# Seven half products for the down projections of two of three SwiGLU groups, in one sequence with the up pairs

## What is computed

```python
def swiglu(x, wg, wu, wd):
    hid = jax.nn.silu(jnp.einsum('btd,df->btf', x, wg)) * jnp.einsum('btd,df->btf', x, wu)
    return jnp.einsum('btf,fd->btd', hid, wd)

x = layer_norm(ALPHA * x + 0.5 * swiglu(x, ffn1_wg, ffn1_wu, ffn1_wd), ln1_g, ln1_b)
...
x = layer_norm(ALPHA * x + 0.5 * swiglu(x, ffn2_wg, ffn2_wu, ffn2_wd), ln3_g, ln3_b)
```

## Time and profile before

| | us |
|---|---|
| median of 3 runs (1088.27 to 1089.12) | 1088.27 |
| the profiled execution's own time | 1087.43 |
| its span | 1085.6 |
| TensorE matmul busy (8731 matmuls) | 1054.4 |
| VectorE busy | 688.7 |
| GpSimd busy | 525.6 |
| ScalarE busy | 437.2 |

### The profile page before, as it was taken

How to read it: one execution, slowest core, us unless ns; L and a number is a source line. 1 busy time by engine, 2 the same in 40 slices (tenths; PEclk the granted TensorE clock), 3 DMA queues, 4 the chain that set the end, 5 groups by cost and what they waited for, 6 DMA issues and landing times.

```text
span 1085.6 us, 20864 instructions
## 1 busy us (share of the span) xinstructions
PE 1054.4 (97%) x8731; PEld 1047.7 (97%) x8731; DVE 688.7 (63%) x1019; ACT 437.2 (40%) x658; POOL 525.6 (48%) x311
## 2 busy tenths in 40 slices
PE   8899999999999988999999999989999999999996
PEld 7899999999999988999999999988999999999996
DVE  6999921288846865342625427989996016886486
ACT  4565532155553443222231324445555113555234
POOL 4355654154568246444453546324565433566321
PEclk9999999999999999999999999999999999999999
DMA  8134234233355042242342335103334323433402
GB/s 256 36 102 117 77 100 117 78 100 116 98 137 136 15 108 75 68 117 72 90 117 67 114 93 144 40 2 97 114 94 125 88 69 98 117 99 88 121 26 79
DMA packets 195002, 103.30 MB, mean 95 GB/s; under 512 B 4420, under 2 KB 193428, under 8 KB 194901
## 3 DMA queue, kind: packets, MB, share of 16 engines
q1 hardware_dynamic: 194827, 101.85, 33.0%
q10 hardware_dynamic: 82, 0.12, 0.1%
HBM read 99.74 MB, written 2.48 MB: 94 GB/s over the span
## 4 chain that ended last, share of the span: by engine, by line
PE 85%; DVE 10%; issue 2%; ACT 2%; DMA 1%; POOL 0%; SPq 0%; ACTq 0%; DVEq 0%; POOLq 0%
PE ps L1303 14%; PE ps L1323 14%; PE ps L1320 14%; PE ps L1321 14%; PE ps L1305 14%; PE ps L1304 14%; DVE x L1179 1%; DVE xl L925 1%; DVE x L1160 1%; DVE form_lo L976 1%; DMA raw<-in_ffn_wd_dram 1%; DMA xrow<-in_x_prompt_dram 1%; PE ps L1426 1%; PE ps L1366 1%; PE ps L1416 0%
## 5 line engine op out<-in xcount | busy, mean ns | idle before, releaser
L569 POOL TENSOR_TENSOR wl<-raw,wh 128x512 fp32r<-128x512 f32 x120 | 221.6, 1874 | 226.2 <-DVE raw L951 182.3
L615 ACT ACTIVATE wh<-raw 128x1024 fp32r<-128x1024 f32 (+3 forms) x203 | 238.4, 1178 | 191.9 <-DMA raw<-in_ffn_wd_dram 102.2
L1303 PE MATMUL ps<-form_hi,wh 128*128 128x260 f32 x640 | 182.3, 285 | 5.1 <-ACT temps L615 5.1
L1305 PE MATMUL ps<-form_hi,wl 128*128 128x260 f32 x640 | 181.6, 284 | 0.0
L1304 PE MATMUL ps<-form_lo,wh 128*128 128x260 f32 x640 | 181.6, 284 | 0.0
L1320 PE MATMUL ps<-xh,wh 128*128 128x260 f32 x640 | 167.9, 283 | 3.8 <-DVE ymix L1253 3.8
L1321 PE MATMUL ps<-xl,wh 128*128 128x260 f32 x640 | 167.3, 283 | 0.0
L561 POOL TENSOR_TENSOR wl<-raw,wh 128x1536 fp32r<-128x1536 f32 (+2 forms) x36 | 108.1, 3010 | 107.1 <-ACT wh L615 107.1
L1320 PE MATMUL ps<-hid_hi,wh 128*128 128x260 f32 x544 | 141.9, 282 | 0.0
L1321 PE MATMUL ps<-hid_lo,wh 128*128 128x260 f32 x544 | 141.8, 283 | 0.0
L1303 PE MATMUL ps<-xh,wh 128*128 128x260 f32 x480 | 136.8, 285 | 2.1 <-DVE temps L983 1.5
(11 more groups left out here) (225 smaller groups left out, 2354.7 us busy)
## 6 DMA issues: line engine op xcount, KB each, us to landing
raw<-in_ffn_wg_dram SPq DMA_DIRECT2D x80, 256.0 KB, 3.3
raw<-in_w_in_dram SPq DMA_DIRECT2D x40, 512.0 KB, 3.9
raw<-in_ffn_wd_dram SPq DMA_DIRECT2D x16, 768.0 KB, 5.7
b<-in_ffn_wu_dram SPq DMA_DIRECT2D x40, 256.0 KB, 3.4
raw<-in_ffn_wu_dram SPq DMA_DIRECT2D x40, 256.0 KB, 3.0
raw<-in_ffn_wd_dram SPq DMA_DIRECT2D x16, 640.0 KB, 5.4
raw<-in_w_out_dram SPq DMA_DIRECT2D x7, 512.0 KB, 3.9
xrow<-in_x_prompt_dram SPq DMA_DIRECT2D x4, 512.0 KB, 5.3
```

What stands on the lines that cost most here:

```text
L569: nc.gpsimd.tensor_tensor(wl_slot[:, s, :], raw_slot[:, s, :], wh_slot[:, s, :].bitcast(F32), ALU.subtract).then_inc(lo_ready, 1)
L615: return nc.scalar.activation(out, in_, ACT.Copy)
L1303: mm(out, hi, vh, start=start and n == 1, stop=False, skip_group_check=more)
L1305: ins = mm(out, lo, vh, start=False, stop=n == count, skip_group_check=more)
```

## The change

The 22 hidden tiles form three groups of 8, 6 and 8. The down products of the first two groups become units of the same form as the up pairs: a unit takes two output tiles (2j, 2j+1) and treats the group's even and odd hidden tiles as the two halves of the inner dimension. Seven half products of four blocks (group 0) or three (group 1) take the place of eight. Up pairs and down units stand in one list, `UNITS`, of NU = 28, numbered p: 1 to 7 are hidden tiles 2 to 8; 8 to 11 the down units of group 0; 12 to 17 hidden tiles 9 to 14; 18 to 21 the down units of group 1; 22 to 28 hidden tiles 15 to 21. One stream of two slot sets serves all of them. The last group's down products stay full, with 8 blocks a chunk; chunks are placed in two slots and split in two halves by GpSimd.

For the down units the moving operands are made from hidden tiles in VectorE's turns: hid_hi and hid_lo become several tensors (one, two, mid, late, and the second token half of xh and xl for the fourth form, with its fp32 in xl32, which now has memory of its own), and `mid_sums` and `mid_rest` make the forms of tiles 1 to 7 and 9 to 13. The results go straight into x32 (`down_first`, `down_second`, `down_fourth`), where the copies kept by ScalarE carry the 0.5. Silu is one ScalarE instruction, and the products L983, L1012 and L1016 are gone. ScalarE rounds T1 and T3 first, then the loaded blocks, then T2 and T4; before it was the loaded blocks, then T1 and T3, then T2 and T4. The scaling of the residual is spread by SCALED_IN. In the diff the first `unit_steps` is ScalarE's and the second VectorE's.

```diff
-    SPANS = ((2, 12), (12, KF))
-    HELD = (12, KF - 12)
+    GROUPS = (8, 6, 8)
+    UNITS = [None]
+    for g in range(len(GROUPS)):
+        for f in range(max(GROUP_AT[g], 2), GROUP_AT[g] + GROUPS[g]):
+            UNITS.append(("up", f))
+            if g and f == GROUP_AT[g]:
+                UNITS += [("down", g - 1, j) for j in range(K // 2)]
...
         def in_halves(what):
-            return what[0] in ("mix", "out") and size_of(what) == K
+            return (what[0] in ("mix", "out") or what[1] == "down") and size_of(what) >= 6
...
+            def load_unit(n, p):
+                if UNITS[p][0] == "up":
...
+                else:
+                    _, g, j = UNITS[p]
+                    k0, k1 = GROUP_AT[g], GROUP_AT[g] + GROUPS[g]
+                    b11, b21 = (column(wd_v[n], 2 * j)[:, k0 + i:k1:2, :] for i in range(2))
+                    b12_, b22 = (column(wd_v[n], 2 * j + 1)[:, k0 + i:k1:2, :] for i in range(2))
+                load_half(n, "B11", p, b11)
+                if unit_no(n, p) > 2:
+                    sp.wait_ge(t13_made, unit_no(n, p) - 2)
...
                 def hid_up(f, pair):
                     act.wait_ge(s.hid_made, f + 1)
-                    copy(two(hid_hi[:, f % HELD[0], :]), pair_of(pair)).then_inc(s.hid_round, 1)
+                    if f == 0:
+                        act.wait_ge(w_used, number[n, "open", 3])
+                    i = (f - GROUP_AT[group_of(f)]) // 2
+                    if group_of(f) < LAST_GROUP and f % 2 == 0:
+                        copy(one_hi[:, one_at(f), :], bank(pair, 0))
+                        ins = copy(even32[:], pair_of(pair))
+                    elif group_of(f) < LAST_GROUP:
+                        ins = copy(two_hi[:, :, i, :], pair_of(pair))
...
+                def unit_steps(p):
...
+                    act.wait_ge(w_used, number[n, "P1", p])
+                    keep(first_p, x_bank, 1, p_taken)
+                    act.wait_ge(w_used, number[n, "Q5", p])
+                    keep(first_q, z_bank, 1, q_taken)
+                    if p < NU:
+                        round_thirteen(n, p + 1)
...
+                    if was[0] == "up":
+                        second_gate(p - 1)
+                    if p < NU:
+                        round_unit(n, p + 1)
...
+                    act.wait_ge(w_used, number[n, "P6", p])
+                    keep(first_u, x_bank, -1, u_taken)
+                    if was[0] == "up":
+                        hid_up(was[1], p % 2)
+                    if p < NU:
+                        round_twenty_four(n, p + 1)
+                    if was[0] != "down":
+                        round_mid(was[1])
+                    if not down:
+                        act.wait_ge(p_taken, no)
+                        nc.scalar.activation(bank((p + 1) % 2, 0), gate_sum, ACT.Silu).then_inc(s.on1, 1)
...
+            SCALED_IN = {2: (0, 1), 4: (2, 3), 6: (4,), 8: (5,), 9: (6,), 10: (7,)}
...
+                def fourth_sum(i):
+                    return tt(half(xl32[:, i, :], 1), even32[:, 0, :], even32[:, 1, :], ALU.subtract)
+
+                def mid_sums(f, pair):
+                    i = (f - GROUP_AT[group_of(f)]) // 2
+                    dve.wait_ge(s.hid_round, f + 1)
+                    if f % 2 == 0:
+                        fourth_sum(i).then_inc(s.mid_made, 1)
+                        return
+                    first = step.on(tt(mid32[:, 0, i, :], even32[:, 1, :], bank(pair, 1), ALU.subtract))
+                    if i == 0:
+                        fourth_sum(i)
+                    dve.wait_ge(s.mid_step, first)
+                    second = step.on(tt(mid32[:, 1, i, :], mid32[:, 0, i, :], even32[:, 0, :], ALU.subtract))
+                    dve.wait_ge(s.mid_step, second)
+                    tt(mid32[:, 2, i, :], mid32[:, 1, i, :], bank(pair, 0), ALU.add).then_inc(s.mid_made, 1)
...
+                def down_first(p):
...
+                    a, b = half(x32[:, 2 * j, :], 0), x32[:, 2 * j + 1, :]
+                    tt(a, a, first_p, ALU.add).then_inc(p_taken, 1)
+                    tt(b, b, first_uq, ALU.add).then_inc(u_taken, 1)
...
+                    stt(a, bank(q, 0), 0.5, a, ALU.mult, ALU.add)
...
+                    stt(b, bank(2, q), 0.5, b, ALU.mult, ALU.add).then_inc(s.part, 1)
...
+                def unit_steps(p):
+                    was, now = UNITS[p - 1] or ("open", 1), UNITS[p]
+                    if was[0] == "up":
+                        up_second(p - 1)
+                    elif was[0] == "down":
+                        down_second(p - 1)
...
+                    if p < NU:
+                        weight_sums(n, p + 1)
+                        if not even:
+                            rest_thirteen(n, p + 1)
+                    if was[0] == "up":
+                        hid_pair(p - 1)
+                    elif was[0] == "down":
+                        down_fourth(p - 1)
+                    if p < NU and even:
+                        rest_thirteen(n, p + 1)
+                    if f in MID_NO and f % 2:
+                        if f - 1 in MID_NO:
+                            mid_rest(f - 1)
+                        mid_sums(f, pair)
+                    if was[0] == "up":
+                        hid_rest(f, pair)
+                    if f in MID_NO and f % 2 == 0:
+                        mid_sums(f, pair)
+                    if p < NU:
+                        rest_twenty_four(n, p + 1)
+                    scale_residual(2 * n, SCALED_IN.get(p, ()))
+                    if now[0] == "up":
+                        gate_first(p)
+                        up_first(p)
+                    else:
+                        down_first(p)
+                    if f in MID_NO and f % 2:
+                        mid_rest(f)
...
                 def fourth(p):
+                    pe.wait_ge(t24_ready, unit_no(n, p))
+                    pe.wait_ge(q_taken, unit_no(n, p))
+                    half_product("Q4", "T4", p, bank((p + 1) % 2, 1), start=False)
```

More of the change, by code:

```diff
@@ new lines, in half_product, with fourth, second @@
+                def half_product(name, weight, p, out, start=True):
+                    done(run(out, [(block_of((n, weight, p), k), *moving(name, p, k)) for k in range(kblocks(p))],
+                             start=start, more=not start), n, name, p)
+                def fourth(p):
+                    pe.wait_ge(t24_ready, unit_no(n, p))
+                    pe.wait_ge(q_taken, unit_no(n, p))
+                    half_product("Q4", "T4", p, bank((p + 1) % 2, 1), start=False)
+                def second(p):
+                    pe.wait_ge(lo_ready, lo_no[n, "B21", p])
+                    half_product("P2", "B21", p, bank((p + 1) % 2, 0))
```

754 lines of the change are left out of this document (394 added, 360 removed).

## The result

The changed kernel takes **1122.43 us** (median; 1120.43 to 1122.84), the kernel before 1088.27 in the same job: ratio 1.0309, 95% interval 1.0291 to 1.0326. The forecast was 1112, the range 1075 to 1130. So it is slower, by 34 us where 24 were forecast. The profiled execution spans 1120.3 us against 1085.6.

What follows compares the result with a forecast made beforehand. TensorE, busy 97%, was taken to bound the kernel before. Terms -20.2 - 1.2 + 42.8 + 6.0 = +27.4 on 1087.4 gave 1114.8, lowered to 1112 us because bounds reach further down; range 1075 to 1130.

Steps and rivals of the forecast that it cites:

- The bound moves to VectorE: FFN units 2 to 8: VectorE turns of about 11.5 us, where TensorE needs 10.08.
- Blocking as the cause: Unit turns: VectorE instructions reading two SBUF operands wait for GpSimd's reads, whatever their size; 1.9 us per odd turn.
- The overrun's size: Units of both FFNs: VectorE's turns exceed TensorE's time by 21.4 us per FFN, +42.8 us; bounds nothing and 60.
- No idle time in VectorE: Units 2 to 8: VectorE runs without idle, in turns of 11.5 us where pairs took 10.1.
- DMAs: nothing: FFN weight loads: 24 more issues cost nothing, or up to 1 us in each of four short units.
- The norm, +6: Closing stage and norm: TensorE waits 4 us in the first and 2 in the last, +6; bounds 0 and 14.
- some 3: Closing stage: splitting in halves on GpSimd (1.3 us) returns some 3 us to VectorE.
- The start, -1.2: Before the first unit: two VectorE gate products go, the first hidden tile comes sooner, -1.2 us once.
- A: Units 2 to 8, odd turns: TensorE stays the bound and the change keeps its gain, 1072 us; chance 0.19.
- B: FFN units: the overrun is half, GpSimd's instructions slipping into idle before hid_rest, 1093 us; chance 0.13.
- C: Unit turns: stalls of 1.5 us lower the granted clock in 15 turns, 25 us more, 1137 us; chance 0.08.
- Matmuls, -20.2: Down products of groups 0 and 1: 168 fewer matmuls at 0.120 us each, -20.2 us.

Runs made afterwards that it cites:

- 7: Even slots and scaling on ScalarE, plus B22's rest on VectorE: 1101.20 us; separately, changed kernel without P7's third pass in units 2 to 8: 1122.44 us.
- 3: Changed kernel with GpSimd writing zeros instead of subtracting for the rests of B11, B21 and B22: 1080.58 us, ratio 0.9925.
- experiment 6: GpSimd writes zeros for the three loaded rests: changed kernel with even slots 1069.98 us, ratio 0.9826; kernel before 1083.96 us, ratio 0.9962.
- 5: Changed kernel with each mix and out chunk reusing the seventh chunk back's slot: 1107.72 us; also with the residual's scaling on ScalarE: 1100.96 us.
- 8: Changed kernel with even slots and scaling on ScalarE: loaded factors rounded earlier in even turns, 1102.18 us; or 780-column rest one turn later, 1110.55 us.

## Why the prediction was right, and where it was not

**The bound moves to VectorE: right, and shown.** TensorE relieved of 56 matmuls gained nothing (7); with GpSimd's reading gone the kernel gained 38 to 42 us (3, 6).

**Blocking as the cause: right, and shown**, at 260 columns as well as at 1024. With it gone from both kernels the units exceed 0.120 a matmul by 4.8 + 7.2 us in the changed one and by 1.1 + 3.0 in the one before. So of the 38.9 us by which the overrun grew, 7.9 stay without GpSimd's reading, and 31 are blocking and the waits that it brings on. 20.2 less 7.9 is 12.3, near the 14 that experiment 6 measured as the change's worth.

**The overrun's size: right by two faults that cancel.** Forecast 42.8, measured in the units 24.5 + 25.0 = 49.5, so the term was sized 6.7 too low. By unit, over 0.120 a matmul in the first and the second FFN, in us:

| units | first | second | forecast |
|---|---|---|---|
| 1 | 3.0 | 4.1 | 1.0 |
| 2 to 8 | 9.7 | 9.2 | 10.2 |
| 9 to 11 | 2.2 | 2.2 | 2.9 |
| 12 to 17 | 3.3 | 3.3 | 3.2 |
| 18 to 21 | 4.2 | 4.2 | 4.1 |
| 22 to 28 | 2.0 | 2.0 | none |

What is missing lies in unit 1 and in unit 22, the first after the three-block units, which took 11.7 us; the six after it took 10.09 each, light as forecast. (By its own turns, 9.5 + 7.8 + 7.8 + 9.0 against 4 x 7.56, the term for 18 to 21 would be 3.9.) VectorE's turns of units 2 to 8 in the first FFN were 11.0, 11.4, 10.9, 11.1, 10.6, 11.1 and 12.4 against the 11.5, 11.6, 11.5, 11.6, 11.2, 11.6 and 11.8 of the working, 78.5 against 80.8. The failed step is the base: the turns were set against 10.08 us as if the kernel before kept to it, while its own pairs and inner downs exceeded it by 10.6. What counts is 49.5 - 10.6 = 38.9, against 42.8 - 1.2 forecast. The first sum of the earlier trace rows was read where TensorE had no break; the FFN's first turns were not in it.

**No idle time in VectorE: half wrong.** It waits 0.56 us for ScalarE (0.8 was forecast), and 0.66 for TensorE to leave a T4 slot, which no step named. Blocked time per odd turn is 1.2 us (0.55 on L1118, 0.66 on L1108) where 1.9 were reckoned.

**"DMAs: nothing": the failed step with the largest price, +11.0.** The prediction followed the FFN's loads past the queues and left out that the diff also renumbers the slots of mix and out chunks. A transfer's start is set by the last reader of its slot. Four chunks back instead of seven put out chunk 3's load behind mix chunk 47, a rounding before a sigmoid in ScalarE's queue, and TensorE behind that. With the distances restored it is gone (5).

**The norm, +6: wrong.** The last down products lost 11.6 us each time, all that 96 matmuls are worth, and the stages behind them grew by 0.9 and 0.6. VectorE did not become the bound there, because what the working named as returned ("some 3") was enough. VectorE and GpSimd after, the groups that answer to the earlier trace rows:

```profile
L1274 DVE TENSOR_TENSOR temps<-temps 128x520 f32<-128x520 f32 x3 | 4.2, 1402 | 0.0
```

```profile
L618 POOL TENSOR_TENSOR wl<-raw,wh 128x512 fp32r<-128x512 f32 x5 | 7.1, 1421 | 5.1 <-ACT wh L676 5.1
```

The sums took 1.40 us each instead of 2.85, since GpSimd's splits are 1.4 us long and no longer 3.18.

**The start, -1.2: not seen.** TensorE's longest wait in the first turns is 2.7 us after, 2.8 before, and the start as a whole varies by 3.4 us between profiles with the same first instructions.

**The rivals.** A and B put the overrun at nothing or half; it was neither. C, the clock, did not come from the turns as it was forecast: in the units breaks of up to 1.9 us (between two matmuls' starts, beyond 0.12) left the granted clock at 1.00, and its low stretches were not 15 but one in each FFN's units. These came behind the longest breaks there, of 2.9 us (ended at 60.3, low from 61.8) and 2.5 us (ended at 761.0, low from 761.5); a break of 2.8 us that ended at 772.6 was followed by none. The others lie outside the units, the long one at the 8.5 us wait, where no rival looked. Together they are the 8.8 us above, at most: a part of C's 25 came true, at other places. Matmuls, -20.2: right.

So the spans' difference of 34.6 is -20.2 + 38.9 + 11.0 + 1.5 for the stages behind the FFNs and 3.4 for the others, nearly all of it in the start, where the clock differs between profiles. The mechanism was right; that the sum came so near is partly luck, since a missing stall was partly made up by a norm that cost nothing.

## What to carry to other kernels

When work is moved from a full engine to one that is nearly full, cost its instructions beside their neighbours, not by themselves: a 260-column sum was 0.42 us alone and 1.18 beside GpSimd, and, with the slots put right, the blocking alone turned 14 us of gain into 20 of loss. Set every forecast of a stage against what that stage takes today, not against its ideal. And read each renumbered buffer as a change of when its transfer may start: list, for each chunk, how many chunks back its slot was last read, and who stands in the queue behind its wait.

## What the runs showed of the hardware

- A GpSimd instruction that only writes does not hold VectorE up: 168 zeroings per kernel, and VectorE's instructions with two SBUF operands that start while one runs stay at 0.42 us (260 columns) and 1.23 (1024).
- For 512 columns GpSimd takes 1.3 us and VectorE 0.69 by itself; with both at it, VectorE's own instruction took 1.78 (7). Which of the two was given the work made no difference to the time of this kernel (1100.96 and 1101.20 us).
- The blocking moves with the order: releasing GpSimd earlier (8) changed which VectorE instructions were stopped, and their sum rose from about 1.1 to 2.6 us in that turn.
- In and behind one wait of 8.5 us the granted clock was 0.53 over 11 us, while breaks of up to 1.9 us in the units left it at 1.00. Of three breaks of 2.5 to 2.9 us in the first turns of the two FFNs, two were followed by 3.4 us at 0.50 and one was not. Which breaks are followed by a low stretch stays open, and so does whether GpSimd instructions shorter than 512 columns would block less in all.
